# Two-tower transformer on one NeuronCore: the first two attention units of each layer of the first tower started among the fourier matmuls

## The reference, cut to what matters

```
zx, zc = modulate(rms_norm(x or ctx)) @ w_in      # split: f (256), cq (256), ckv (128), kr (32), g (512)
y_f    = Re(fft2(f over tokens and group channels)) @ w_fourier        # "fourier"
q      = rms_norm(cq) @ w_uq;  rope on 32 of 96 columns of each head   # 8 heads
k, v   = rms_norm(ckv) @ w_ukv                                         # keys: context + latents
attn   = softmax(q k^T / sqrt(96)) v              # latents see 768 keys, context (layer 0 only) its 256
y_c    = silu(layer_norm(depthwise_conv31(glu(g)))) @ w_pw2            # "taps": 31 shifts
x      = x + gate * concat(y_f, attn, y_c) @ w_o
```

## Time and profile before

| what | value |
|---|---|
| median of 3 runs | 2952.99 us (2952.99 to 2955.57) |
| profiled execution: its time / its span | 2959.36 us / 2957.6 us |
| PE / DVE / ACT / POOL busy | 94% / 56% / 37% / 38% |
| mean granted clock | 0.973 |
| layer 0, first y matmul to first matmul of scores(2) | 154.42 to 205.95 us |
| layer 1, the same | 1083.27 to 1128.69 us |

### The profile page before, as it was taken

How to read it: one execution, slowest core, us unless ns; L and a number is a source line. 1 busy time by engine, 2 the same in 40 slices (tenths; PEclk the granted TensorE clock), 3 DMA queues, 4 the chain that set the end, 5 groups by cost and what they waited for, 6 DMA issues and landing times.

```text
span 2957.6 us, 38752 instructions
## 1 busy us (share of the span) xinstructions
PE 2786.4 (94%) x14160; PEld 2211.4 (75%) x14160; DVE 1669.5 (56%) x2332; ACT 1099.1 (37%) x1757; POOL 1113.5 (38%) x533
## 2 busy tenths in 40 slices
PE   6988999999999999999999998899999999899998
PEld 3845677888888755678887686577888889688886
DVE  3967696454636567685577653765643642543143
ACT  3335613131212335632233522573433433343242
POOL 1399122323333267044444321003444434244442
PEclk9989999999999999999999998999999999999999
DMA  7500043322323220044444221002543532233332
GB/s 276 204 3 1 1 162 111 127 100 100 128 99 128 85 93 1 30 149 152 161 170 151 83 65 36 1 2 72 193 169 128 199 114 86 71 92 100 94 98 71
DMA packets 82408, 303.63 MB, mean 103 GB/s; under 512 B 9072, under 2 KB 10608, under 8 KB 81392
## 3 DMA queue, kind: packets, MB, share of 16 engines
q1 hardware_dynamic: 82000, 298.43, 29.8%
q10 hardware_dynamic: 288, 3.55, 0.3%
HBM read 299.84 MB, written 2.10 MB: 102 GB/s over the span
## 4 chain that ended last, share of the span: by engine, by line
PE 56%; DVE 5%; ACT 2%; issue 2%; POOL 0%; DVEq 0%; ACTq 0%; POOLq 0%
PE psum L1740 15%; PE psum L1554 10%; PE psum L1244 9%; PE psum L1761 8%; PE psum L1283 3%; PE psum L1648 2%; PE psum L1440 1%; PE psum L1663 1%; PE psum L1264 1%; PE psum L1681 1%; PE psum L1456 1%; PE psum L1626 1%; PE psum L1470 1%; DVE hidden_lo L2175 1%; PE psum L1407 0%
## 5 line engine op out<-in xcount | busy, mean ns | idle before, releaser
L584 POOL TENSOR_TENSOR w_lo<-w_raw,w_hi 128x1024 fp32r<-128x1024 f32 x346 | 864.0, 2497 | 1803.0 <-ACT w_hi L650 1802.8
L650 ACT ACTIVATE w_hi<-w_raw 128x1024 fp32r<-128x1024 f32 x346 | 366.9, 1061 | 1271.4 <-PE psum L1554 548.5
L1896 DVE SCALAR_TENSOR_TENSOR residual<-psum,modulation,residual 128x512 f32<-128x512 f32 (+1 forms) x168 | 111.6, 684 | 382.7 <-PE psum L1554 189.5
L1915 DVE CUSTOM_DVE_ANT_0 mod_w<-mod_w,conditions 128x1024 f32<-128x1024 f32 x176 | 287.4, 1642 | 4.4
L1740 PE MATMUL psum<-in_hi,w_hi 128*128 128x512 f32 x672 | 261.8, 390 | 2.6 <-DVE small_w L2390 1.6
L1740 PE MATMUL psum<-in_hi,w_lo 128*128 128x512 f32 x672 | 261.4, 389 | 0.0
L1740 PE MATMUL psum<-in_lo,w_hi 128*128 128x512 f32 x672 | 261.4, 389 | 0.0
L1244 PE MATMUL psum<-in_hi,w_hi 128*128 128x512 f32 (+1 forms) x704 | 237.9, 377 | 6.9 <-DVE in_lo L2450 3.9
L1554 PE MATMUL psum<-hidden_hi,w_hi 128*128 128x512 f32 (+1 forms) x768 | 231.0, 355 | 2.6 <-DVE hidden_lo L2175 2.2
L1554 PE MATMUL psum<-hidden_lo,w_hi 128*128 128x512 f32 (+1 forms) x768 | 230.3, 354 | 0.0
L1244 PE MATMUL psum<-in_hi,w_lo 128*128 128x512 f32 (+1 forms) x704 | 230.2, 366 | 0.0
(11 more groups left out here) (271 smaller groups left out, 5453.9 us busy)
## 6 DMA issues: line engine op xcount, KB each, us to landing
w_raw<-stream_dram SPq DMA_DIRECT2D x346, 512.0 KB, 4.2
mod_w<-mods_dram SPq DMA_DIRECT2D x176, 512.0 KB, 3.6
mixer_space<-first_mods_dram SPq DMA_DIRECT2D x12, 512.0 KB, 15.2
small_w<-small_w_dram SPq DMA_DIRECT2D x2, 2048.0 KB, 12.3
in_hi_space<-dft_x_dram SPq DMA_DIRECT2D x2, 2048.0 KB, 8.9
residual<-tokens_dram ACTq DMA_DIRECT2D x1, 3072.0 KB, 10.8
in_lo_space<-first_mods_dram SPq DMA_DIRECT2D x4, 512.0 KB, 15.4
conditions<-conditions_dram SPq DMA_DIRECT2D x2, 1024.0 KB, 10.2
```

Source lines behind the costliest of these rows:

```text
L584: nc.gpsimd.tensor_tensor(wlo[:, (j % 2) * 1024:(j % 2 + 1) * 1024], raw3[:, j, :], whi[:, (j % 2) * 1024:(j % 2 + 1) * 1024].bitcast(F32) ...
L650: nc.scalar.activation(whi[:, (j % 2) * 1024:(j % 2 + 1) * 1024], raw3[:, j, :], ACT.Copy).then_inc(hi_ready, 1)
L1896: last = nc.vector.scalar_tensor_tensor(res3[:, m, s0:s1], bank(2 * (t % 2) + b, c1=s1 - s0), M(block_, chunk, m, 1 - b), res3[:, m, s0:s1 ...
L1915: nc.vector.tensor_tensor_reduce(w_tile, w_tile, cvec[:, 0:D], 1.0, 0.0, ALU.mult, ALU.add, dots[:, q:q + 1]).then_inc(mod_done, 1)
```

## The change

What it does, for both layers of the first tower:

- y gets memory of its own: `yf`, the first 1536 columns of `l_f`, in place of `zf` (= `qbuf`). It lies where f_lo writes later, so f_lo now waits until both f sums are done (`f_mm` >= 2).
- y and f both lie in banks 3 to 6 (`fourier_out`: 3 and 4 for latents, 5 and 6 for context). Banks 0 to 2 are left for scores, 7 for projections.
- The ab stage holds a projection behind every piece but the first: P0 to P4 in layer 0, P0 to P2 in layer 1. The rest of the early ones is dealt to the pieces of y (`early_pieces`): P5, P6, P7 ahead of the first three of four in layer 0; P3 and P4 ahead of the first of two and P5 ahead of the second in layer 1.
- scores(0) stands behind the first half of y, scores(1) behind f. The loop no longer issues these two, nor minimum(0), exps(0) and weigh(0), which move ahead of the end of y or f.
- f goes c by c, so that its first half waits for the first copy of y only.
- DVE's taps are set by `TAPS_BEFORE`: in layer 0 11 ahead of rope_q(0), 1 more ahead of rope_q(1), 2 ahead of minimum(0), 1 ahead of weigh(0), 6 ahead of f_lo, 10 in the loop (before 7). In layer 1 15 ahead of the query norm as before, 15 ahead of rope_q(0), the last behind it; weigh(0) and rope_q(1) come ahead of f_lo.

No matmul, copy or DMA is added or taken away; POOL's and SP's lists are the same.

```diff
+        yf = l_f[:, 0:2 * T].rearrange("p (k t) -> p k t", k=2)
...
-        EARLY_TAPS = ((0, 24), (15, TAPS))
+        TAPS_BEFORE = [dict(queries=0, rope0=11, rope1=12, minimum=14, weigh=15, fourier=21),
+                       dict(queries=15, rope0=30, minimum=TAPS, weigh=TAPS, rope1=TAPS, fourier=TAPS)]
+        def fourier_out(m, seg):
+            return bank(3 + m if seg == LAT else 5 + m, c1=w(seg))
+        def early_pieces(layer, slots):
+            toks = 6 if layer == 0 else 4
+            todo = list(range(toks - 1, 8 if layer == 0 else 6))
+            each = -(-len(todo) // slots)
+            return [todo[each * i:each * i + each] for i in range(slots)]
...
 # ScalarE
-                    if 1 <= i <= 3:
+                    if i:
                         proj_ev(i - 1)
...
+                segs = both(cols)
+                pieces = early_pieces(layer, 2 * len(segs))
+                for c in range(2):
+                    for _ in segs:
+                        for n in pieces.pop(0):
+                            proj_ev(n)
+                    if c:
+                        exps(0)
+                    act.wait_ge(s["y_mm"], c + 1)
+                    for seg, _ in segs:
+                        last = nc.scalar.activation(yf[:, c, seg[0]:seg[1]], fourier_out(c, seg), ACT.Copy)
+                    last.then_inc(s["y_cp"], 1)
...
 # TensorE
+                for c in range(2):
+                    for seg, _ in segs:
+                        for n in pieces.pop(0):
+                            project(n)
+                        if c == 0:
+                            pe.wait_ge(late["dft"], 32 * (layer + 1))
...
+                    mm.then_inc(s["y_mm"], 1)
+                    if c == 0:
+                        scores(0)
+                for m in range(2):
+                    for c in range(2):
+                        if m == 0:
+                            pe.wait_ge(s["y_cp"], c + 1)
+                        for seg, _ in segs:
+                            mm = pe.matmul(fourier_out(m, seg), wf[:, m, c, :],
+                                           yf[:, c, seg[0]:seg[1]], start=(c == 0), stop=(c == 1))
+                    mm.then_inc(s["f_mm"], 1)
+                scores(1)
+                pe.wait_ge(s["f_lo"], 2)
...
                 for d in range(n_units + 1):
-                    if d + 1 < n_units:
+                    if d and d + 1 < n_units:
                         scores(d + 1)
...
 # VectorE
+                steps = dict(rope0=lambda: rope_q(0), rope1=lambda: rope_q(1),
+                             minimum=lambda: minimum(0), weigh=lambda: weigh(0))
+                for step, until in TAPS_BEFORE[layer].items():
+                    if step in steps:
+                        taps(until)
+                        steps[step]()
+                taps(TAPS_BEFORE[layer]["fourier"])
+                dve.wait_ge(s["f_mm"], 2)
```

More of the change, by code:

```diff
@@ L1399, in _ @@
                 pe.wait_ge(s["ab_cp"], len(toks))
[L1400 to L1408, removed]
-                                                  256 * c + 128 * part + 128],
-                                               table[:, part, k, :], start=(k == 0 and part == 0),
-                                               stop=(k == nk - 1 and part == 1))
-                    mm.then_inc(s["y_mm"], 1)
-                pe.wait_ge(s["y_cp"], 2)
-                pe.wait_ge(sa["proj_act"], 4)
-                for m in range(2):
-                    for seg, b in both(cols):
-                        for c in range(2):
-                            mm = pe.matmul(bank(m if b else 6 + m, c1=w(seg)), wf[:, m, c, :],
-                                           zf[:, c, seg[0]:seg[1]], start=(c == 0), stop=(c == 1))
-                    mm.then_inc(s["f_mm"], 1)
-                pe.wait_ge(s["f_lo"], 2)
-                first = min(behind.values())
-                half = 4 + (first - 4) // 2
-                for n in range(4, half):
-                    project(n)
                 def scores(u):
@@ L2034, in _, with taps @@
                     dve.wait_ge(drained[i], (t0 + 6) // 2)
-                for k in range(EARLY_TAPS[layer][0]):
-                    tap(k)
+                taken = [0]
+                def taps(until):
+                    for k in range(taken[0], until):
+                        tap(k)
+                    taken[0] = until
+                taps(TAPS_BEFORE[layer]["queries"])
                 dve.wait_ge(s["lora_sums"], 2)
@@ L2042, in _ @@
                                                    ALU.mult, ALU.mult).then_inc(s["lora_ready"], 1)
-                for k in range(*EARLY_TAPS[layer]):
-                    tap(k)
-                for m in range(2):
-                    dve.wait_ge(s["f_hi"], m + 1)
-                    for seg, b in both(cols):
-                        last = nc.vector.tensor_tensor(lo3[:, m, seg[0]:seg[1]],
-                                                       bank(m if b else 6 + m, c1=w(seg)),
-                                                       hi3[:, m, seg[0]:seg[1]].bitcast(F32),
-                                                       ALU.subtract)
-                    last.then_inc(s["f_lo"], 1)
                 sa = att[layer]
@@ L2132, in _ @@
                         for k in range(rest * d // tap_loops, rest * (d + 1) // tap_loops):
-                            tap(EARLY_TAPS[layer][1] + k)
+                            tap(early + k)
                     for x in ln_stages(layer, d):
```

41 lines of the change are left out of this document (30 added, 11 removed).

## The result

| | before | after |
|---|---|---|
| median of 5 executions | 2952.99 us (2952.77 to 2955.57) | 2933.55 us (2926.34 to 2938.22) |
| profiled execution: time / span | 2959.36 / 2957.6 | 2935.03 / 2933.2 |
| mean granted clock | 0.973 | 0.983 |

The ratio is 0.9927, with a 95% interval of 0.9909 to 0.9945: faster by 19.4 us, where 31 were forecast. 2933.55 lies above the range of 2915 to 2931. The executions of the changed kernel also lie 12 us apart, those of before 3.

The account below looks back on a forecast made before the run. It took PE, busy 94% of the span, as the bound, with time to win only in its gaps and low-clock stretches. 15.5 (layer 0) + 15.4 (layer 1) = 30.9, say 31: 2952.99 becomes 2922, range 2915 to 2931.

Parts of the forecast that it names:

- Part 2: Layer 0's attention, walked in the new order at full clock: scores(2) starts at 190.4 instead of 205.95, gain 15.5 us.
- DVE's margin: Layer 0, ahead of f_lo: DVE finishes its taps only 0.3 to 1 us before f is done.
- Rival (a): DVE late in layer 0 by one or two taps, 1.6 to 3 us: gain 24 to 28, 2927; chance 0.15.
- Part 3: Layer 1's attention, walked in the new order: scores(2) at 1113.3 instead of 1128.69, gain 15.4 us.
- Part 4: Clock behind the 2.7 us gap at layer 0's scores(2): taken as low (5.46 us), nothing gained; other end 2.7 us more.
- Part 5: Layer 0's loop: three more DVE taps hide in idle time, cost 0; other end 4.8 us if none hides.
- POOL: Layer 0's convolution taps on POOL end at 310.0; PE reaches the layer norm 4 to 7 us behind.
- rival (b): POOL's taps become slower and PE waits ahead of the layer norm: 6 us lost at 2.9 us each, 2928; chance 0.06.
- The rule that the prediction weighed: Layer 0: DVE instructions with two SBUF inputs and GpSimd ones reading SBUF exclude each other; sum left unchanged.
- (c): Only one layer gains, because an unseen wait puts scores(1) back behind a chain: 2937; chance 0.06.
- (d): Slower than before: the loop stays at 1.2 GHz after the 2.7 us gap; 50 us of such work gives 2972; chance 0.03.
- (e): The clock stays up at layer 0's scores(2): 2.7 us more gain, 2919; chance 0.66 together with the forecast.

Follow-up runs that it names:

- even: The changed kernel with layer 0's MLP tiles cut into 384 + 384 columns in place of 256 + 512: 2926.4 us.
- nudge_all: The changed kernel with the first matmul of 62 of the 64 tiles of layer 0's MLP issued twice: 2929.9 us in one execution.
- b_even: The kernel before with layer 0's MLP tiles cut into 384 + 384 columns: 2953.9 us.
- the pairs: Changed kernel against kernel before, both with layer 0's MLP segments in turned order, or both cut into 384 + 384 columns: gains of 26.3 and 26.8 us.
- after_again: The changed kernel run once more, nothing edited: 2929.9 us.
- l1_only: The changed kernel with the old order put back in layer 0, so the new order in layer 1 alone: 2946.9 us, ratio 0.996 to before.

## Why the prediction was wrong

- **What bounds the kernel: right.** The gain did come from PE's gaps and its stretches at the low clock.
- **Part 2, layer 0: right for the trace it was read from.** 44.95 us from ab to scores(2) against 60.93 are 16.0 us; 15.5 were walked. P4's gap was 1.38 (1.3), f ended at 183.6 (184.5), scores(2) came at 189.28 (190.4).
- **DVE's margin: too pessimistic.** 2.16 us were left ahead of f_lo, not 0.3 to 1, since its six taps took 8.87 us, 1.48 each, where 1.56 were counted, and the ropes less than the bound of 3.2 us. Rival (a) didn't come.
- **Part 3, layer 1: right in the same sense.** 53.27 less 37.54 are 15.7 us; 15.4 were walked.
- **Part 4, the clock behind scores(2): neither end.** The list of gaps that it was read from left out the one of 1.38 us, which was followed by matmuls of double length too. The 2.65 us gap was there, and scores(2) took 4.54 us between the 2.75 and 5.46 that I had named. Which value comes depends on the execution: from first to last start its matmuls take 2.25 us in even's trace and 4.43 in nudge_all's, behind the same 44.95 us.
- **Part 5, the loop: right.** From scores(2) to the layer norm's first matmul 126.3 us before and 125.4 after. The three more taps cost nothing.
- **POOL: too optimistic.** In after's trace it ended at 312.9, not 310, and PE came at 314.70, 1.8 us behind it and not 4 to 7. In even's trace, with the same program up to there, rival (b) came true, for 3.2 us of wait. "The same 31 taps" was not so: in before's trace 29 of them start ahead of POOL's end, in the changed kernel's all 31, and POOL's taps took 170.2 us where they took 167.4 (172.3 in even's trace). The rule that the prediction weighed, of the Trainium skill, "SBUF — State Buffer", section "Who interferes with whom", agrees with the direction of this; no run isolates it.

```profile
311.68 1.19 POOL L630 TENSOR_TENSOR mixer_space<-mixer_space 128x392 f32<-128x392 f32 x1
...
314.70 1.88 PE L1501 MATMUL psum<-mixer_space,ones 128*128 128x512 f32 x4
```

- **The sum: here it failed, in two ways.** The first is the step from the two stages to the end of the kernel. "Sum: 15.5 + 15.4" carried the gain through all that follows as if a stretch in which PE never waits took a fixed time. Layer 0's MLP doesn't: it takes 537.5 or 547.3 us, by a cadence that a start behind a wait can draw anew. Before's first trace had the fast one, the changed kernel's the slow one. For the executions without a trace the cadence is an estimate from their times: b_even, which can't have the 1060 ns, took 2949.0 or more, so before would take 2958.7 or more with them, and none of its five did; even took 2923.8 or more, so the changed kernel takes 2933.5 or more with them, and three of its five did. The median of the changed kernel thus has the 1060 ns in it, and that of before the 1040: up to 10 of the missing 11.6 us, which belong to neither kernel. In means the gain was 21.5 us (2953.8 less 2932.3); with three fifths of 9.7 us added it is 27.3, close to the 26.5 of the pairs. Against 2959.4 the trace should have come at 2928; it came at 2935.0, and with an MLP of 537.5 us in place of 547.0 it would be 2925.5.
- **The second is a term that was mis-sized**: the cost of the old chain was taken from one execution, in which the low clock cost nearly the most that it ever does. Over five traces each, the old stages take 58.9 and 52.5 us, so the mean gain of the stages is 13.9 + 15.0 = 28.9 us, not 31.7 as in the first pair of traces. Measured with the cadence out, the gain is 26.5, give or take 2. That the two differ is within the error. One us of it may be chance in the last stretch, from DVE's last product with the rope table in the second tower to the end: the five traces with the old layer 1 take 1171.7 us there in the mean, the nine with the new one 1172.8. Behind one and the same wait of 4.42 us in it, the clock comes back sooner or later by the execution, for 1.5 us, in one program too. Windows of after's trace and of after_again's:

```profile
2555.00:2558.00 3.00, 3.00 (x8) 2.08 (x7) 2.93 (x6) 1.45 (x3) 0.00 (x0) 0.50 0.00 0
```

```profile
2555.00:2558.00 3.00, 3.00 (x13) 1.96 (x12) 2.93 (x5) 1.54 (x3) 0.00 (x0) 0.97 0.00 0
```

- **The rivals.** (c), 2937, came nearest to the time and is wrong in its mechanism: both layers gained. (a) and (d) did not occur; (b) did in even's trace; (e) in part, as said under Part 4.
- **The range** had 2 us for the spread of the executions, from three executions of before. It is 16 to 19 us for both kernels. With the slow cadence's 10 us on top of 2922 and the rival (a) behind it, the upper end would have had to be near 2940.

## What to carry to other kernels

A gain that was walked in one stage is paid out at the end only if the stages behind it have one speed, so the same landmarks (here three transfers) should be compared in both traces before any cause is looked for in the change. A stage in which PE never waits and which alternates lengths should be timed in several executions; here the cut into equal pieces cost nothing (537.5 us) and took most of the spread out. Hiding a chain of small waits is worth the chain's mean cost, which one trace doesn't give: a chain that lets the clock fall now and then takes another time in each execution.

## What was not expected of the hardware

- Alternating matmuls of 256 and 512 columns, with a weight load each and at a granted clock of 1.00, run at either 1040 or 1060 ns for three pairs. A stream without waits keeps its cadence (over 520 us, and the fast one over 62 matmuls put in); behind a wait either may come (9 and 7 of 16 stretches in one trace). The order 256, 512, 512, 256 runs at 1045, 384 + 384 at 1040.
- In the slow cadence the three products are unequal, 395, 398 and 403 ns, and which weights get the 403 varies: in_lo by w_hi in the changed kernel, in_hi by w_lo in l1_only:

```profile
L1630 PE MATMUL psum<-in_hi,w_lo 128*128 128x512 f32 x156 | 62.9, 403 | 0.0
```

- The same gaps of 4.13 and 3.04 us were followed by score groups of 5.46 and 5.49 us in one execution and 4.51 and 4.18 in another; layer 1 in the new order, whose longest gap is 0.77 us, agrees to 0.01 us in nine traces.
